# Side work of VectorE moved between slots, and three sets of loads moved ahead in SyncE's queue

## The chip, the cores and the metric

The kernel runs on one core of a Trainium2 chip. The metric is the device time of one execution in microseconds (us), the median of several runs. Engines: PE is TensorE, DVE is VectorE, ACT is ScalarE, POOL is GpSimd, SP is SyncE, which here only issues DMAs.

## The reference, cut to what matters

Two transformer-like blocks run one after the other on a sequence of 2048 tokens of width 1024, in float32. The change lies in the first block. It normalises x, projects it (`w_in`), and feeds one part of the projection to windowed attention and another, `u_ssm` (512 channels in 32 groups of 16), to a linear recurrence in both directions:

```
lam, dt  = a_re + i*a_im, exp(log_dt)
a_bar    = exp(lam * dt)
b_bar    = (b_re + i*b_im) * (a_bar - 1) / lam
xs       = scan(x_t = a_bar * x_{t-1} + b_bar u_t)      # 64 states a group, 2 directions
y       += Re(xs) c_re - Im(xs) c_im                      # plus d * u
```

## The kernel before, in words

All engines run programs written out by hand, with semaphores. Each engine works strictly in the order of its own program; SP, ACT and POOL also issue the DMAs.

**First projection (st).** `te_st` computes u and the gates by a seven-product scheme: 20 steps q = 0 to 19, each with products P1, P5, P6, P7, P2, P3, P4 of four 128x128 by 128x512 matmuls. P3 waits for the combination `c22` of the same step on DVE, P2 for `p1` of the same step on ACT. `ve_st` does for each q: `u2`, `c22` (two additions, u3 and c22), four sums of weights for q+1, side slot 2q, `c12`, `c21`, side slot 2q+1. So whatever stands in a side slot delays the combinations behind it. ACT makes gates of step q (behind c12 and c21), issues a weight load for q+2, and then makes p1 of q+1.

**Side slots.** `ve_side(v, s)` fills slot s with preparation of the recurrence: in slots 2 to 8 the parameters, the last of it the "turns" (`ve_prm_turns`, eleven rounds of up to ten small operations, each dependent on the one before), then eight quarters of matrices (`ve_mat`, quarter q4 in slots MAT_AT[q4] to +2, steps 0, 1, 2). Step 0 makes b1 and b2, step 1 six products for outputs and three for inputs, step 2 the other nine; step 2 ends with the event QA of the quarter. SP then stores the quarter to `pwd` in three DMAs (`sp_mat`), and loads coefficients of quarter q4+2 into the buffer BCs. `te_lag` multiplies 16 small matmuls of a quarter at the end of step q = LAG_AT[q4]; it waits for QA. `ac_lag` and `ve_lag` finish them (slot 2*LAG_AT[q4]+2), and SP stores them to `hkd`. POOL waits for the end of the turns and then makes the rotations (`po_rot`, 16 pairs of groups, about 34 us each), and stores them to `rotd`.

**Recurrence (s5).** For 32 groups g: `te_s5_first` transposes a loaded pwd matrix, `te_s5_states` multiplies it with Ug (u laid out by group, loaded from `ud` by `sp_ug`, m = 0 to 3 for eight groups each, eight copies of 128 KB a call), DVE rotates with the loaded rotation (`ve_s5_states`, L1170), scans, rotates back (`ve_s5_gates`, L1185), and `te_s5_out` multiplies the result. Late tiles of another projection (`te_proj`, weights loaded by ACT) are spread between the groups. SP issues all loads and stores of the stage in program order, `sp_s5`.

Of the kernel before, what the change touches and what calls it, by code (L numbers as in the profile page):

```python
# [23 lines left out]
TAILS = [48, 51, 54]  # L24
SP_, UT = 10, 4
SQ = 2 * SP_
MAT_AT = [9, 12, 15, 20, 23, 26, 29, 32]
LAG_AT = [6, 7, 10, 12, 13, 15, 16, 18]


class Counts:
# [62 lines left out]
def build(nc, T, out):  # L94
    ctx = ExitStack()
    with ctx:
# [5 lines left out]
        def reg(kb, *shape):  # L102
            o = int(round(kb * 256))
            n = 1
            for x in shape:
                n *= x
            assert o + n <= 207 * 256, (kb, shape)
            v = arena[:, o:o + n]
            if len(shape) == 2:
                v = v.rearrange("p (a b) -> p a b", a=shape[0])  # L110
            if len(shape) == 3:
                v = v.rearrange("p (a b c) -> p a b c", a=shape[0], b=shape[1])
            return v
# [472 lines left out]
        def ve_side(v, s):  # L586

            if s == 1:
                ve_bias(v)
            if s == 2:  # L590
                ve_prm_angle(v)
            if s == 4:
                ve_prm_coef(v)
            if s == 5:
                ve_prm_powers(v)
            if s == 6:
                ve_prm_turns(v, 0, 4)
            if s == 7:
                ve_prm_turns(v, 4, 8)
            if s == 8:  # L600
                ve_prm_turns(v, 8, 11)
            for q4 in range(8):
                if s == 2 * LAG_AT[q4] + 2:
                    ve_lag(v, q4)
            for q4 in range(8):
                if 0 <= s - MAT_AT[q4] < 3:
                    ve_mat(v, q4, s - MAT_AT[q4])

# [298 lines left out]
            s.do.dma_start(dst, pj_stage(n)).then_inc(*dma(f"st_sg{n % 2}", "pj", n))  # L907


        BCs = [reg(166.5, 4, 8, 16), reg(173.5, 4, 8, 16)]  # L910
        BAs = reg(175.5, 4, 256)
        CA2 = [reg(180, 4, 288), reg(114, 4, 288)]
        QAs = reg(184.5, 4, 288)
# [23 lines left out]
            s.do.dma_start(BCs[q4 % 2].rearrange("p a b c -> p (a b c)"), T["bc"][q4]).then_inc(*dma(f"ld_bc{q4 % 2}", "bc", q4))  # L937

        def sp_mat(s):
            sp_mat_load(s, 0)  # L940
            s.wait_ge(*at("prm_ve", "turns"))
            sp_mat_load(s, 1)
            for q4 in range(8):
                dst = pwd[4 * q4:4 * q4 + 4]
                s.wait_ge(*at("mat_ve", "QA", q4))
                s.do.dma_start(dst[:, :, 0:256].rearrange("g p n -> p g n"), BAs).then_inc(*dma("st_pw0", "pw", q4))
                s.do.dma_start(dst[:, :, 256:544].rearrange("g p n -> p g n"), CA2[q4 % 2]
                               ).then_inc(*dma("st_pw1", "pw", q4))
                s.do.dma_start(dst[:, :, 544:832].rearrange("g p n -> p g n"), QAs).then_inc(*dma("st_pw2", "pw", q4))
                if q4 + 2 < 8:  # L950
                    sp_mat_load(s, q4 + 2)
                if q4:
                    sp_lag(s, q4 - 1)
                if q4 in (2, 3):
                    sp_st_u(s, SP_ + q4 - 2, 0)
                    sp_st_u(s, SP_ + q4 - 2, 1)
            sp_lag(s, 7)
# [27 lines left out]
        def ve_lag(v, q4):  # L985
# [5 lines left out]
            tt(v, q, o, o, bank(7)[0:16, :].rearrange("p (g n) -> p g n", g=4)[:, :, 112:128], ADD)  # L991
            tt(v, q, o, o, dd, ADD, "H", q4)

        def ve_mat(v, q4, step):
            q = "mat_ve"
            c8_ = slice(8 * q4, 8 * q4 + 8)
            B1, B2, C1, C2 = (BCs[q4 % 2][:, k, :, :] for k in range(4))
            CAs, b1, b2, x2 = CA2[q4 % 2], b1s[q4 % 2], Bb[:, 0, :, :], Bb[:, 1, :, :]
            if step == 0:
                v.wait_ge(*at("prm_ve", "turns"))  # L1000
                v.wait_ge(*at(f"ld_bc{q4 % 2}", "bc", q4))
                v.wait_ge(*at("ld_sgn", "sgn"))
                v.wait_ge(*at("ld_dcol", "dcol"))
                ts(v, q, B2, B2, sgn[:, 1:2], None, MUL, BYP)
                ts(v, q, C1, C1, sgn[:, 0:1], None, MUL, BYP)
                ts(v, q, C2, C2, -1.0, None, MUL, BYP)
                cr, ci = bc(coef[:, 0, c8_], 2, [128, 8, 16]), bc(coef[:, 1, c8_], 2, [128, 8, 16])
                v.wait_ge(*at("side_pe", "H", q4 - 2))
                tt(v, q, b1, B1, cr, MUL)
                tt(v, q, x2, B2, ci, MUL)  # L1010
                tt(v, q, b1, b1, x2, ADD)
                tt(v, q, b2, B2, cr, MUL)
                tt(v, q, x2, B1, ci, MUL)
                tt(v, q, b2, b2, x2, SUB)
            if step == 1:
                pw_stored(v, q4 - 1)
                ve_mat_inputs(v, q4, 0)
                if q4 == 1:
                    v.wait_ge(*at("side_pe", "bias", 7))
                ve_mat_outputs(v, q4, 0)  # L1020
            if step == 2:
                ve_mat_inputs(v, q4, 1)
                ve_mat_outputs(v, q4, 1, "QA", q4)
# [268 lines left out]
        def sp_s5(s):  # L1292
            sp_ug(s, 0)
            for g in range(3):
                sp_s5_pw(s, g)
            sp_s5_blocks(s, 0)
            sp_s5_rot(s, 0)
            sp_s5_rot(s, 1)
            for n in LATE[0]:
                sp_proj(s, n)  # L1300
            for g in range(G):
# [13 lines left out]
                    sp_s5_channels(s, g)  # L1315
                for n in LATE[4 * g + 4]:
                    sp_proj(s, n)
                if g < 3:
                    sp_ug(s, g + 1)

# [2350 lines left out]
```

## Time and profile before

| what | value |
|---|---|
| median of 3 runs | 3506.26 us (3501.18 to 3506.35) |
| the profiled execution's own time | 3506.26 us |
| its span, first to last instruction | 3504.5 us |
| TensorE busy | 3373.6 us, 96% |
| VectorE busy | 1810.0 us, 52% |
| ScalarE, GpSimd busy | 1030.6 and 1151.2 us |
| mean granted TensorE clock | 0.989 |

Busy time counts instructions at work, not waits. The granted clock is a share of 2.4 GHz. The st stretch ends at 552.8 us, the recurrence follows.

### The profile page before, as it was taken

What the parts mean: (1) busy time and instruction counts of PE and PEld (TensorE: products, weight loads), DVE (VectorE), ACT (ScalarE), POOL (GpSimd) and SP (SyncE); (2) the same over time, 40 slices, a digit from 0 to 9 for tenths busy, and PEclk for the clock granted to TensorE, in tenths of its full rate; (3) what the DMA queues carried; (4) which work ended last, traced back from release to release, by engine and by line L of the source; (5) the groups of instructions that cost most, each with busy time, mean ns of one, the idle gap of its engine ahead of it and who ended that gap; (6) DMA issues with size and microseconds to landing.
All of it is one profiled execution on the core that took longest, in us unless ns stands there. A gap on an engine that the chain in (4) does not pass through costs nothing.

```text
span 3504.5 us, 32439 instructions
## 1 busy us (share of the span) xinstructions
PE 3373.6 (96%) x10992; PEld 1716.6 (49%) x10992; DVE 1810.0 (52%) x4003; ACT 1030.6 (29%) x2527; POOL 1151.2 (33%) x1499
## 2 busy tenths in 40 slices
PE   7999998999999999999999999999999996999998
PEld 4444444555445544444444445555664443444443
DVE  6778774665454773325565557744454554222222
ACT  3321222222100660002234446643332222322322
POOL 3087786750000890000000003655651001344342
PEclk9999999999999999999999999999999997999999
DMA  4344448655263103222221000000102226978885
GB/s 152 114 161 134 172 151 236 185 169 160 104 205 125 37 25 121 107 84 96 72 80 33 24 13 10 1 1 1 73 25 92 102 89 230 349 193 273 253 249 135
DMA packets 133161, 423.60 MB, mean 121 GB/s; under 512 B 20661, under 2 KB 60469, under 8 KB 116830
## 3 DMA queue, kind: packets, MB, share of 16 engines
q1 hardware_dynamic: 93388, 226.42, 19.3%
q0 software_dynamic: 31392, 153.50, 14.0%
q10 hardware_dynamic: 8208, 41.53, 3.4%
q8 instruction: 90, 1.47, 0.2%
q14 instruction: 83, 0.68, 0.1%
HBM read 354.96 MB, written 121.62 MB: 136 GB/s over the span
## 4 chain that ended last, share of the span: by engine, by line
PE 84%; DVE 8%; ACT 3%; DMA 2%; issue 1%; POOL 0%; SPq 0%; ACTq 0%; DVEq 0%; POOLq 0%
PE pst L145 55%; PE pst L383 10%; PE pst L150 6%; DVE arena L167 4%; PE pst L2619 3%; PE pst L2714 3%; PE pst L2622 2%; PE pst L1679 1%; DMA arena<-rotd 1%; PE pst L1594 1%; ACT arena L156 1%; PE pst L1152 1%; ACT arena L2459 1%; DVE arena L173 1%; DVE arena L170 1%
## 5 line engine op out<-in xcount | busy, mean ns | idle before, releaser
L145 PE MATMUL pst<-arena 128*128 128x512 f32 (+5 forms) x5290 | 2140.3, 560 | 22.9 <-DVE arena L1185 11.5
L145 PEld LDWEIGHTS pst<-arena 128*128 128x128 f32 (+1 forms) x5290 | 971.8, 191 | 1040.7 <-issue 999.1
L383 PE MATMUL pst<-arena 128*128 128x512 f32 x1120 | 489.3, 595 | 9.4 <-DVE arena L167 6.8
L167 DVE TENSOR_TENSOR arena<-arena 128x512 f32<-128x512 f32 (+9 forms) x897 | 455.1, 509 | 64.6 <-ACT arena L2660 19.6
L167 POOL TENSOR_TENSOR arena<-arena 128x4 f32<-128x4 f32 (+7 forms) x784 | 435.8, 556 | 81.4 <-DVE arena L2423 21.0
L150 PEld LDWEIGHTS pst<-arena 128*128 128x128 f32 x2080 | 244.3, 143 | 214.6 <-issue 149.3
L150 PE MATMUL pst<-arena 128*128 128x128 f32 x2080 | 310.1, 281 | 39.5 <-DVE arena L257 15.1
L383 PEld LDWEIGHTS pst<-arena 128*128 128x128 f32 x1120 | 211.4, 190 | 273.1 <-issue 253.4
L1647 POOL TENSOR_SCALAR arena<-arena 128x384 f32<-128x384 f32 (+1 forms) x128 | 151.5, 1202 | 399.2 <-DVE arena L1639 398.0
L156 ACT ACTIVATE arena<-pst,arena 128x128 f32<-128x128 f32 (+1 forms) x638 | 237.5, 470 | 138.0 <-PE pst L150 134.9
L2603 POOL TENSOR_SCALAR arena<-arena 128x512 f32<-128x512 f32 (+3 forms) x160 | 218.3, 1384 | 147.2 <-DVE arena L167 137.1
L173 DVE SCALAR_TENSOR_TENSOR arena<-arena 128x512 f32<-128x512 f32 (+4 forms) x438 | 198.2, 452 | 37.1 <-ACT arena L2122 19.4
L176 ACT ACTIVATE arena<-arena 128x1024 f32<-128x1024 f32 x64 | 67.6, 1056 | 502.3 <-DVE arena L1899 350.1
L173 DVE SCALAR_TENSOR_TENSOR arena<-arena,pst 128x256 f32<-128x256 f32 x96 | 43.3, 451 | 327.1 <-ACT arena L3344 325.4
L170 DVE TENSOR_SCALAR arena<-arena 128x1 f32<-128x1 f32 (+10 forms) x601 | 157.4, 262 | 95.2 <-ACT arena L2118 39.9
L155 ACT ACTIVATE arena<-pst 128x512 f32<-128x512 f32 (+4 forms) x242 | 121.3, 510 | 279.4 <-PE pst L145 112.4
L167 DVE TENSOR_TENSOR arena<-pst,arena 128x512 f32<-128x512 f32 (+2 forms) x156 | 103.3, 662 | 174.8 <-PE pst L383 96.5
L2024 POOL MEMSET arena<- 128x256 f32 x1 | 0.3, 311 | 476.8 <-ACT arena L156 476.8
L161 DVE COPY arena<-pst 128x512 f32<-128x512 f32 (+2 forms) x202 | 108.7, 545 | 79.1 <-PE pst L150 35.1
L2638 DVE TENSOR_REDUCE arena<-pst 128x2 f32<-128x1024 f32 (+2 forms) x80 | 85.3, 1066 | 114.2 <-PE pst L2622 113.1
L2714 PE MATMUL pst<-arena 128*128 128x256 f32 (+1 forms) x576 | 142.7, 371 | 1.2 <-DVE arena L161 1.2
L2654 ACT ACTIVATE arena<-pst,arena 128x512 f32<-128x512 f32 (+3 forms) x160 | 98.3, 619 | 143.0 <-DVE arena L2638 141.5
(217 smaller groups left out, 2407.6 us busy)
## 6 DMA issues: line engine op xcount, KB each, us to landing
arena<-in_w_ada SPq DMA_DIRECT2D x48, 512.0 KB, 4.7
arena<-in_w_ug ACTq DMA_DIRECT2D x18, 1024.0 KB, 6.0
sgd<-arena ACTq DMA_DIRECT2D x32, 512.0 KB, 3.4
rotd<-arena POOLq DMA_DIRECT2D x32, 512.0 KB, 4.7
arena<-rotd SPq DMA_DIRECT2D x32, 512.0 KB, 4.6
arena<-sgd SPq DMA_DIRECT2D x16, 1024.0 KB, 7.1
arena<-pwd SPq DMA_DIRECT2D x32, 416.0 KB, 5.8
arena<-in_x SPq DMA_DIRECT2D x18, 512.0 KB, 4.3
```

The lines of the kernel that those rows point to most:

```text
L145: x = t.do.matmul(o, l, r, start=(i == 0), stop=(i == len(pairs) - 1))
L150: x = t.do.transpose(o, i, ident[0:i.shape[0], 0:i.shape[0]])
L155: return a.do.activation(o, i, ACT.Copy)
L156: return a.do.activation(o, i, ACT.Identity, bias=0.0 if bias is None else bias, scale=1.0 if scale is None else scale)
L161: return v.do.tensor_copy(o, i)
L167: own(v, s).tensor_tensor(o, a, b, op).then_inc(*inc(s, *event))
L170: own(v, s).tensor_scalar(o, a, s1, s2, o1, o2).then_inc(*inc(s, *event))
L173: own(v, s).scalar_tensor_tensor(out=o, in0=a, scalar=sc, in1=b, op0=o1, op1=o2).then_inc(*inc(s, *event))
L383: x = t.do.matmul(st_bank(q, i), left[:, k, :], right[:, k, :], start=(name in FIRST and k == 0), stop=(k == 3), skip_group_check=name != ...
L1647: p.do.tensor_scalar(P_x, P_x, es[:, c:c + 1], None, MUL).then_inc(*inc("win_po", *(["P", j] if x == 3 else [])))
L2603: p.do.tensor_scalar(P_x, P_x, ff[:, r % 4, x, c:c + 1], None, MUL).then_inc(*inc("mla_po", "P", n, x))
L2714: last_ = t.do.matmul(bank(6 + x)[:, w], V2[:, 2 * hp + x, j, :], PT2[n % 4][:, 256 * l:256 * l + 256][:, w], start=(j == 0), stop=(j == 2 ...
```

## The change

The turns go into slots 6 and 7 instead of 6, 7 and 8. MAT_AT changes, so quarter 0 starts in slot 8 and quarters 5 to 7 one slot later; LAG_AT is computed from it and becomes 6, 8, 9, 12, 13, 15, 17, 18. The three input products of direction 0, and the wait for the stores of the quarter before, move from step 1 to step 0. The two buffers of coefficients change places, and the load of quarter 0 waits for the turns. In SP's program for s5 the Ug loads 1 and 2 are issued ahead of the first two rotation loads and Ug 3 right behind them, instead of after groups 0, 1 and 2.

```diff
-MAT_AT = [9, 12, 15, 20, 23, 26, 29, 32]
-LAG_AT = [6, 7, 10, 12, 13, 15, 16, 18]
+MAT_AT = [8, 12, 15, 20, 23, 27, 30, 33]
...
             if s == 6:
-                ve_prm_turns(v, 0, 4)
+                ve_prm_turns(v, 0, 6)
             if s == 7:
-                ve_prm_turns(v, 4, 8)
-            if s == 8:
-                ve_prm_turns(v, 8, 11)
+                ve_prm_turns(v, 6, 11)
...
-        BCs = [reg(166.5, 4, 8, 16), reg(173.5, 4, 8, 16)]
+        BCs = [reg(173.5, 4, 8, 16), reg(166.5, 4, 8, 16)]
...
         def sp_mat(s):
+            s.wait_ge(*at("prm_ve", "turns"))
             sp_mat_load(s, 0)
-            s.wait_ge(*at("prm_ve", "turns"))
             sp_mat_load(s, 1)
...
+        LAG_AT = [(m + 2) // 2 + 1 for m in MAT_AT]
...
                 tt(v, q, b2, b2, x2, SUB)
-            if step == 1:
                 pw_stored(v, q4 - 1)
                 ve_mat_inputs(v, q4, 0)
+            if step == 1:
                 if q4 == 1:
                     v.wait_ge(*at("side_pe", "bias", 7))
                 ve_mat_outputs(v, q4, 0)
...
             sp_s5_blocks(s, 0)
+            sp_ug(s, 1)
+            sp_ug(s, 2)
             sp_s5_rot(s, 0)
             sp_s5_rot(s, 1)
+            sp_ug(s, 3)
             for n in LATE[0]:
                 sp_proj(s, n)
...
                 for n in LATE[4 * g + 4]:
                     sp_proj(s, n)
-                if g < 3:
-                    sp_ug(s, g + 1)
```

## Rows read from the trace of the kernel before

**Rows 1.** The page, part 1: busy us, share of the span, instructions.

```profile
PE 3373.6 (96%) x10992; PEld 1716.6 (49%) x10992; DVE 1810.0 (52%) x4003; ACT 1030.6 (29%) x2527; POOL 1151.2 (33%) x1499
```

**Rows 2.** PE's waits in 110 to 552 us: total us, times, longest.

```profile
PE pst L383 <- DVE arena L167: 2.9, 3, 1.4
PE pst L383 <- ACT arena L155: 1.9, 1, 1.9
PE pst L972 <- DVE arena L167: 1.8, 1, 1.8
```

**Rows 3.** PE's waits in 552 to 720 us.

```profile
PE pst L145 <- DVE arena L1185: 8.6, 2, 6.8
PE pst L1152 <- ACT arena L155: 5.2, 7, 1.5
PE pst L150 <- DMA arena<-pwd: 3.6, 1, 3.6
```

**Rows 4.** PE's timeline: start, us, instructions, idle before and releaser.

```profile
244.16 1.92 PE L972 MATMUL pst<-arena 128*16 128x128 f32 x16 [1.75 <-DVE arena L167]
...
363.07 7.13 PE L383 MATMUL pst<-arena 128*128 128x512 f32 x16 [1.45 <-DVE arena L167]
...
466.00 10.57 PE L383 MATMUL pst<-arena 128*128 128x512 f32 x24 [1.87 <-ACT arena L155]
```

**Rows 5.** DVE and weight loads, 143 to 158 us; then L167 in one window.

```profile
143.53 1.49 DVE L167 TENSOR_TENSOR arena<-pst,arena 128x512 f32<-128x512 f32 x2
...
154.80 2.28 DVE L167 TENSOR_TENSOR arena<-pst,arena 128x512 f32<-128x512 f32 x3
...
157.14 0.41 PEld L383 LDWEIGHTS pst<-arena 128*128 128x128 f32 x2 [0.44 <-DVE arena L167]
...
160.75:166.39 5.64, 3.52 (x17) 0.00 (x0) 1.00 0.00 0
```

**Rows 6.** PE in 557 us (us, PE busy, clock, DMA share, GB/s), then PE's timeline.

```profile
557.00:558.00 1.00, 1.00 (x2) 0.50 1.04 421
...
556.67 8.73 PE L145 MATMUL pst<-arena 128*128 128x512 f32 x16
...
575.88 4.60 PE L145 MATMUL pst<-arena 128*128 128x256 f32 x10 [6.78 <-DVE arena L1185]
...
580.66 7.03 PE L145 MATMUL pst<-arena 128*128 128x512 f32 x16
...
588.40 2.32 PE L145 MATMUL pst<-arena 128*128 128x256 f32 x10
```

**Rows 7.** SP's queue, timeline from 545 us: start, us, issues.

```profile
545.25 3.66 SPq L661 DMA_DIRECT2D arena<-ud  x8
549.02 1.31 SPq L1106 DMA_DIRECT2D arena<-pwd  x3
...
554.19 0.86 SPq L1112 DMA_DIRECT2D arena<-rotd  x2
```

**Rows 8.** Landing of those two rotation loads, and DVE's timeline.

```profile
DMA to landing us min/median/max: 16.9/17.3/17.7
...
571.08 0.69 DVE L1170 TENSOR_TENSOR arena<-pst,arena 128x512 f32<-128x512 f32 x1 [3.87 <-DMA arena<-rotd]
```

**Rows 9.** A window while Ug 1 loads (last three: clock, DMA share, GB/s); queues in 560 to 572.

```profile
584.50:590.50 6.00, 6.00 (x22) 3.94 (x21) 1.68 (x3) 1.78 (x3) 5.11 (x12) 1.00 1.11 144
...
q10 hardware_dynamic: 239, 2.42, 52.7%
q1 hardware_dynamic: 555, 1.29, 28.6%
```

**Rows 10.** DVE's timeline near 219 and 362 us; landing of three pwd stores at 244.

```profile
219.05 11.72 DVE L167 TENSOR_TENSOR arena<-arena 128x512 f32<-128x512 f32 x9
...
362.33 0.69 DVE L167 TENSOR_TENSOR arena<-pst,arena 128x512 f32<-128x512 f32 x1 [3.40 <-DMA ud<-arena]
...
DMA to landing us min/median/max: 2.9/4.2/7.0
```

## The prediction

> **What bounds the kernel now.** The page's first part comes first: TensorE (PE) is busy for 96% of the span [rows 1]. So a change counts only where it moves a moment at which PE stands still. The change touches two stretches, the first projection (st, up to 552.8 us) and the start of the recurrence (s5, 552.8 to about 620 us). The second view is therefore the table of PE's waits in each [rows 2, 3]. In 110 to 552 us the reader sees 6.6 us that the change can reach: 1.8 for the lag product of quarter 1 (te_lag, L972), 2.9 in three waits of L383 for VectorE (DVE), and 1.9 in one for ScalarE. In 552 to 720 us PE waits 3.6 us for the first pwd load and 8.6 for DVE's gates, 6.8 of it at once. The third view is the timeline around these waits [rows 4 to 6], the fourth SP's queue and what it makes the gates wait for [rows 7 to 9].
>
> **Turns in two slots instead of three.** DVE's side work runs in slots, two for each step q. The change puts turns 4 and 5 into slot 6 and turns 6 to 10 into slot 7; before, the last three turns stood in slot 8, behind u2, u3 and c22 of q = 4. DVE is dense there: c12 and c21 of q = 3 run at 143.53, slot 7 ends as u2, u3 and c22 of q = 4 start at 154.80, these take 2.28 us, and product P3 of q = 4, which waits for c22, loads its weights at 157.14, 0.44 us late already [rows 5]. There is no cover left. The last three turns took 160.75 to 166.39, 5.64 us [rows 5]. They are the same 26 small operations (two rounds of ten and one of six) wherever they stand, so c22 of q = 4 ends 5.6 us later and P3 starts near 162.8: **+5.6 us**. The matmuls before it don't hide this: P2 runs before P3 already, and its own input (p1, which ScalarE makes behind the gates of q = 3) moves by the same 5 us and takes at most a part of the same wait. What is late next is c12 and c21 of q = 4 and sums of q = 5, but slot 8 now holds less that must be done before u2 of q = 5 and PE itself is late, so nothing is added.
>
> A wait of that length costs speed as well. After the 3.6 us wait at 552.8 the granted clock is 0.50, that is 1.2 instead of 2.4 GHz, at 557 us, and 16 records of 128x512 take 8.73 us where 16 at 580.66 take 7.03; after the 6.8 us wait 10 records of 128x256 take 4.60 where 10 at 588.40 take 2.32 [rows 6]. So 1.7 to 2.3 us. After waits of 1.8 us there is none of it: 24 records after the wait at 466.00 take 10.57 us, 0.44 each [rows 4]. The new wait of 4 to 5.6 us is nearest to the first: **+1.8 us**, with 0 and 2.3 as ends (0 if P2 splits it in two).
>
> The first load of the quarters' coefficients now waits for the turns, since its buffer lies on the parameters. It is 256 KB, with u2, u3, c22 and four sums between it and its user, over 5 us, so I put it at nothing; without that cover it would be 1 us, on DVE alone.
>
> **Quarter schedule.** For quarter 1 te_lag moves from the end of q = 7 to the end of q = 8, while its products still end in q = 7: the 1.75 us wait at 244.16 [rows 4] goes, and no later instruction takes it over, because u2 and c22 of q = 8 had 8 us of idle before them. **-1.8 us**. For quarters 3 and later, step 1 gives three of its nine products to step 0. The wait at 466.00 (ScalarE's p1, late because c12 and c21 of q = 15 stood behind the nine products of slot 31) loses the cause: **-1.9**. The three waits for DVE sum to 2.9 us; one of 1.45 is at 363.07, the other two together 1.4. These two go as the slots become shorter: **-1.4**. The one at 363.07 stays, because c22 of q = 12 waits for a store of ud at 362.33 that SP issues behind the quarter's stores [rows 4, 10]: 0, between -1.4 (slot 22 ends earlier) and +1.
>
> The move has a price. Step 0 now waits for pw_stored of the quarter before, and behind this wait stand u2, u3 and c22 of the next q. For quarters 2, 4, 6 and 7 the slot before step 0 is the one that ends the quarter before. The stores take up to 7.0 us from issue to landing [rows 10], and some 8 us with their issue. A product takes 3.5 us (16 records, two products, in 7.13 [rows 4]), and from the end of such a quarter to P3 of the next q PE has about five of them to do (P1, P5, P6, P7, P2), 17 us. The stores land at 8, so DVE's three products end near 10.5, and u2, u3, c22 near 13. It fits at q = 8 and, with a margin below 1 us, at q = 17, where quarter 6 ends late: **+0.3**, between 0 and 6 (four places at 1.5).
>
> Sum of the st stretch: 5.6 + 1.8 - 1.8 - 1.9 - 1.4 + 0.3 = **+2.6 us**.
>
> **The order of SP's loads.** Before, SP issues the eight copies of Ug 0 at 545.25, three pwd loads at 549.02, eight small block loads, and the first two rotation loads at 554.19 [rows 7]. The first rotation lands 16.9 us later, and DVE's first product (L1170) starts at 571.08 having waited for exactly it; DVE's gates end 4.8 us on, and PE starts at 575.88 [rows 6, 8]. The rotation load is thus on the path. The change puts Ug 1 and Ug 2, sixteen copies and 2.1 MB, ahead of it in the same queue. What such copies cost the engines shows where Ug 1 runs before: 584.5 to 590.5 us at 144 GB/s with the DMA engines' share at 1.11 [rows 9], so 1.05 MB takes 7.3 us, and two 14.6 us. That is the upper end. The lower is nothing: between 560 and 572 us SP's queue holds only 28.6% of the engines, and ScalarE's (the 2 MB of za's weights) 52.7% [rows 9], so part of the copies could run in the shadow of that load. But the engines are full all the while (1.04 at 557 us [rows 6]), so most of the copies' time must be added, not hidden; the row nearest to them is their own. If a quarter of the 14.6 us is hidden, 11 us are left. I take **+11 us**, with 5 to 14.6 as its own range. The clock penalty after this wait is already in the profile (2.3 us), so it adds nothing.
>
> The Trainium skill (DMA: Bandwidth & Descriptors, "Queues, rings and completion order") states that each DMA engine takes turns between the queues that have work, a packet at a time. The split of the three queues in this trace agrees; by that rule alone the weights of za don't hold SP's copies back, the delay would be nearer to 5 us than to 14.6, and the whole sum nearer to +8.
>
> Ug 3 goes behind the rotations, and rotation 2 behind it; DVE asks for it a whole group (10 us) after the gates of group 0, which covers 7.3 us. In the loop the three Ug calls disappear, 8 issues each. PE does not wait for any load between 576 and 620 us [rows 3], so their removal gives nothing.
>
> **Sum.** The profiled execution took 3506.26 us (its span 3504.5), which is also the median of the three runs. 3506.3 + 2.6 + 11 = 3519.9, said as **3519.5 us**.
>
> **Rivals.**
> *The Ug copies are hidden (not slower).* If the copies run wholly beside the za weights, the rotation lands when it did: +2.6 us and at most 3 of the rest, 3508 to 3511, within what can be told. For it: SP's share of 28.6%. Against: the engines' share of 1.0 and more in the same stretch. It decides from the point where the first rotation lands before 575 us in the old time frame.
> *DVE runs out of time in the late slots (slower still).* DVE and GpSimd disturb each other: nine products of two SBUF operands took 11.72 us at 219.05, 1.3 us each [rows 10], where a product of the same width at 571.08 takes 0.69 [rows 8]. GpSimd's rotation work starts 6 us earlier and meets DVE in other places. If step 0 comes late at four places, up to 6 us more: 3526. The Trainium skill (SBUF — State Buffer, "SBUF: two separate sides") says that the port pair which the two share is locked by one of them for a whole instruction; the 11.72 us bear it out, and it is as likely to help at one place as to hurt at another.
> *The turns fit (smaller loss).* If PE's wait at q = 4 is nil, the sum is 7.4 lower: 3512. Against it stand 0.44 us of wait already at that point.
> *The lighter queue pays (faster).* With the three Ug calls gone from the loop, PE's short waits for ScalarE in s5 (5.2 us in seven [rows 3]) could shrink. With hidden copies that is 2.6 - 5.2 = -2.6, 3504; it passes the bound of 7 us only if P3 of q = 4 does not wait either (-7.4 more): 3496. Against it: those waits are for a copy of ScalarE, not for a load.
>
> **How the numbers follow.** Forecast 0.60 (3513 to 3527, centre 3519.5), hidden copies 0.20, DVE late 0.10, turns fit 0.05, faster 0.05. Differences under 0.2% (7 us) can't be told from none here. Faster: 0.05. Same: the hidden copies and most of "turns fit", 0.23. Slower: 0.72. The range leaves out the faster case and the top of the two slow ones: 3507 to 3528.
>
> **What the profile after would show.** Right: P3 of q = 4 (with P2 ahead of it) waits 4 to 6 us for DVE near 157 us, with a granted clock of 0.50 behind it; no wait at te_lag of quarter 1; no wait of L383 for ScalarE near 466; L1170's first wait for rotd ends near 584 to 587 us and PE's wait for L1185 is 16 to 19 us instead of 6.8; nothing new between 600 and 900 us. Wrong: a rotation that lands within 20 us of its issue and ahead of the Ug copies, waits on DVE near 260, 363 and 488 us of more than 2 us each, or an end that moves by more than the s5 start does.

## The result

The changed kernel takes 3543.9 us (median of 4 runs, 3534.29 to 3552.55) against 3506.31 us (median of 4, 3501.18 to 3510.79): ratio 1.0109, 95% interval 1.009 to 1.0128, that is 32 to 45 us slower. The forecast was slower, 3519.5 us, with a range up to 3528: the direction was right, and the size, 13 us, was about a third of the 37.6 us that came. The profiled execution took 3544.84 us, its span is 3543.1 us.

The page of the changed kernel, part 1, answers to [rows 1]. PE has 7 us more of busy time (half clock), and the rest of the loss is idle:

```profile
PE 3380.4 (95%) x10992; PEld 1717.4 (48%) x10992; DVE 1811.2 (51%) x4003; ACT 1029.2 (29%) x2527; POOL 1147.4 (32%) x1499
```

PE's timeline of the changed kernel, to be held against [rows 4 to 6]. Columns are start, duration, instructions, and in brackets the idle time before and who ended it. L382 is what was L383, L969 is te_lag, L144 the matrix products of s5:

```profile
155.37 3.70 PE L382 MATMUL pst<-arena 128*128 128x512 f32 x8 [1.16 <-ACT arena L154]
163.80 5.91 PE L382 MATMUL pst<-arena 128*128 128x512 f32 x8 [4.73 <-DVE arena L166]
...
269.62 7.13 PE L382 MATMUL pst<-arena 128*128 128x512 f32 x16 [1.29 <-DVE arena L166]
276.68 1.92 PE L969 MATMUL pst<-arena 128*16 128x128 f32 x16
...
313.46 3.57 PE L969 MATMUL pst<-arena 128*16 128x128 f32 x16 [10.63 <-DVE arena L166]
316.96 73.34 PE L382 MATMUL pst<-arena 128*128 128x512 f32 x168
...
508.27 5.40 PE L382 MATMUL pst<-arena 128*128 128x512 f32 x8 [1.96 <-ACT arena L154]
518.40 9.53 PE L382 MATMUL pst<-arena 128*128 128x512 f32 x16 [4.73 <-DVE arena L166]
...
583.70 0.44 PE L149 MATMUL pst<-arena 128*128 128x128 f32 x2 [3.60 <-DMA arena<-pwd]
...
615.98 3.81 PE L144 MATMUL pst<-arena 128*128 128x256 f32 x10 [19.58 <-DVE arena L1184]
```

From this the loss can be put together, place by place (us):

| place | predicted | in this trace | how |
|---|---|---|---|
| P2 and P3 of q = 4 | +7.4 | +8.2 | 1.16 + 4.73 of wait; 5.91 for 8 records where 8 take 3.60 |
| te_lag of quarter 1 | -1.8 | -1.75 | no bracket at 276.68 |
| P3 of q = 8 (269.62) | 0 | +1.3 | |
| te_lag of quarter 2 (313.46) | 0 | +13.2 | 10.63 of wait; 3.57 instead of 1.92; 73.34 instead of the 72.37 that 168 records take |
| waits at q = 12 to 16 | -3.3 | -4.7 | all four gone |
| P2 and P3 of q = 17 | +0.3 | +10.9 | 1.96 + 4.73; 5.40 instead of 3.60; 9.53 instead of 7.13 |
| first gates of s5 | +11 | +12.0 | wait 19.58 against 6.78; 10 records in 3.81 against 4.60 |
| sum | +13.6 | +39.2 | spans differ by 38.6 |

PE ends the first projection at 580.1 us (583.70 less 3.60) instead of 552.8 and starts the first output product at 615.98 instead of 575.88. Two places, te_lag of quarter 2 and q = 17, show nearly the whole error of the forecast. Where a wait shows is not yet what makes it: the runs below give another sum by parts.

What the two places wait for is in DVE's timeline of the changed kernel:

```profile
294.16 18.60 DVE L166 TENSOR_TENSOR arena<-arena 128x512 f32<-128x512 f32 x17
312.86 0.21 DVE L166 TENSOR_TENSOR arena<-arena,pst 16x64 f32<-16x64 f32 x1
313.10 0.21 DVE L166 TENSOR_TENSOR arena<-arena 16x64 f32<-16x64 f32 x1
...
488.77 12.04 DVE L166 TENSOR_TENSOR arena<-arena 16x64 f32<-16x64 f32 x10
...
513.85 2.30 DVE L166 TENSOR_TENSOR arena<-arena 128x512 f32<-128x512 f32 x3 [8.85 <-DMA pwd<-arena]
```

The two 16x64 operations that end at 313.3 are `ve_lag` of quarter 1, and PE's te_lag of quarter 2 starts at 313.46: it waits for the event H of the quarter before (`side_ve`, "H", q4-1), not for its own products. With LAG_AT 8, `ve_lag` of quarter 1 stands in slot 18, behind the twelve differences T1, T2, T3 and the four sums that are made at q = 9 (17 operations with its own first, 18.6 us). With LAG_AT 9 for quarter 2, te_lag stands at the end of the same step. Near 500 us the three input products, now in step 0, start 8.85 us late because of the stores of quarter 6, and u2 and c22 of q = 17 stand behind them.

SP's queue at the start of s5 (columns as above, durations are of the issuing; answers to [rows 7]), and DVE's first product (to [rows 8]):

```profile
577.61 3.72 SPq L1120 DMA_DIRECT2D arena<-hkd  x8
581.44 15.03 SPq L658 DMA_DIRECT2D arena<-ud  x16
596.57 1.01 SPq L1111 DMA_DIRECT2D arena<-rotd  x2
597.68 9.46 SPq L658 DMA_DIRECT2D arena<-ud  x8
```

```profile
611.12 0.69 DVE L1169 TENSOR_TENSOR arena<-pst,arena 128x512 f32<-128x512 f32 x1 [15.71 <-DMA arena<-rotd]
```

The sixteen copies of Ug hold SP for 15.03 us, twice what 16 issues take when the queue is empty (8 in 3.66 us [rows 7]), so the rotation loads are not only served late but also issued late, at 596.57.

### The profile page after: what moved, and what is told of

Read it like the earlier page. It is cut to its first block, busy times and chain, and to the rows that moved or that the text cites. A ratio compares the mean times of both kernels' runs of the same rounds, so it can differ in the third digit from the quotient of the medians.

```text
span 3543.1 us, 32439 instructions
## 1 busy us (share of the span) xinstructions
PE 3380.4 (95%) x10992; PEld 1717.4 (48%) x10992; DVE 1811.2 (51%) x4003; ACT 1029.2 (29%) x2527; POOL 1147.4 (32%) x1499
## 3 DMA queue, kind: packets, MB, share of 16 engines
q0 software_dynamic: 31392, 153.50, 13.9%
q8 instruction: 90, 1.47, 0.2%
## 4 chain that ended last, share of the span: by engine, by line
PE 82%; DVE 9%; ACT 3%; DMA 2%; issue 1%; POOL 1%; SPq 1%; DVEq 0%; ACTq 0%; POOLq 0%
PE pst L144 54%; PE pst L382 10%; PE pst L149 5%; DVE arena L166 4%; PE pst L2619 3%; PE pst L2714 3%; PE pst L2622 2%; PE pst L1679 1%; DMA arena<-rotd 1%; PE pst L1594 1%; POOL arena L1647 1%; ACT arena L155 1%; DVE arena L169 1%; PE pst L1151 1%; DVE arena L172 1%
## 5 line engine op out<-in xcount | busy, mean ns | idle before, releaser
L144 PE MATMUL pst<-arena 128*128 128x512 f32 (+5 forms) x5290 | 2137.8, 560 | 33.9 <-DVE arena L1184 22.5
L144 PEld LDWEIGHTS pst<-arena 128*128 128x128 f32 (+1 forms) x5290 | 970.3, 191 | 1051.1 <-issue 1010.4
L382 PE MATMUL pst<-arena 128*128 128x512 f32 x1120 | 498.1, 604 | 18.6 <-DVE arena L166 14.7
L166 DVE TENSOR_TENSOR arena<-arena 128x512 f32<-128x512 f32 (+8 forms) x897 | 450.0, 503 | 73.1 <-ACT arena L2660 19.6
L382 PEld LDWEIGHTS pst<-arena 128*128 128x128 f32 x1120 | 214.5, 193 | 288.4 <-issue 257.7
```

The costliest lines, as they stand in the source:

```text
L144: x = t.do.matmul(o, l, r, start=(i == 0), stop=(i == len(pairs) - 1))
L166: own(v, s).tensor_tensor(o, a, b, op).then_inc(*inc(s, *event))
L382: x = t.do.matmul(st_bank(q, i), left[:, k, :], right[:, k, :], start=(name in FIRST and k == 0), stop=(k == 3), skip_group_check=name != ...
```

## The experiments

All differences are against runs of the kernel before on the same chip; its medians there were 3505 to 3506 us.

| run | from | edit | median us | ratio, 95% interval |
|---|---|---|---|---|
| a1_ug | before | SP's order only | 3521.77 | 1.0045 (1.0029 to 1.0062) |
| a2_turns | before | turns in slots 6, 7 only | 3519.66 | 1.0039 (1.0025 to 1.0053) |
| a3_lag89 | before | LAG_AT 8 and 9 for quarters 1, 2 | 3506.09 | 1.0003 (0.9993 to 1.0013) |
| a4_lag79 | before | LAG_AT 7 and 9 | 3506.75 | 1.0002 (0.9992 to 1.0011) |
| b1_lag10 | changed | LAG_AT 8 and 10 | 3536.88 | 1.0093 (1.0077 to 1.011) |
| b2_step1 | changed | input products back in step 1 | 3542.67 | 1.0109 (1.0092 to 1.0125) |
| b3_ugback | changed | SP's order back | 3531.76 | 1.0074 (1.0057 to 1.0091) |
| b4_turns3 | changed | turns in slots 6, 7, 8 | 3522.88 | 1.005 (1.0033 to 1.0066) |
| e1_sched | before | quarter schedule only | 3505.28 | 0.9998 (0.9988 to 1.0007) |
| h1_after_poollate | changed | GpSimd starts later | 3544.42 | 1.0118 (1.0101 to 1.0135) |
| f2_after_zalate | changed | load of za's weights later | 3537.87 | 1.0098 (1.0081 to 1.0115) |
| f1_before_zalate | before | load of za's weights later | 3501.07 | 0.999 (0.9981 to 1.0) |
| d1_s5order | before | another order of SP's loads | 3501.33 | 0.9989 (0.998 to 0.9999) |
| g1_best | before | f1, an order like d1, LAG_AT 8, 10 | 3497.50 | 0.9982 (0.9972 to 0.9992) |
| k1_lag10_ugback | changed | b1 and b3 together | 3523.54 | 1.0057 (1.0043 to 1.0071) |
| k2_turns_lag89 | before | a2 and a3 together | 3523.31 | 1.0054 (1.004 to 1.0067) |

Two further runs leave work out and are read by their first 600 us only.

### The parts alone

**a1_ug.**

```diff
             sp_s5_blocks(s, 0)
+            sp_ug(s, 1)
+            sp_ug(s, 2)
             sp_s5_rot(s, 0)
             sp_s5_rot(s, 1)
+            sp_ug(s, 3)
...
-                if g < 3:
-                    sp_ug(s, g + 1)
```

> Kernel before with only the order of SP's loads changed (Ug 1 and 2 ahead of the first two rotation loads, Ug 3 behind them). Theory: the rotation load waits in SP's queue behind 2.1 MB of copies into 16 partitions each; PE's wait for L1185 at the start of s5 grows from 6.8 to about 19.6 us as in the changed kernel, nothing comes back later: +12 to +13 us. Rival (copies hidden beside the load of za's weights): +0 to +3 us.

+16.3 us by the medians; the interval allows 10 to 22. The first projection is as before, and the wait for the gates is there, so the copies are not hidden. PE's timeline of a1_ug:

```profile
590.81 4.61 PE L145 MATMUL pst<-arena 128*128 128x256 f32 x10 [20.43 <-DVE arena L1185]
```

**a2_turns.**

```diff
             if s == 6:
-                ve_prm_turns(v, 0, 4)
+                ve_prm_turns(v, 0, 6)
             if s == 7:
-                ve_prm_turns(v, 4, 8)
-            if s == 8:
-                ve_prm_turns(v, 8, 11)
+                ve_prm_turns(v, 6, 11)
```

> Kernel before with only the turns in slots 6 and 7, all quarters where they were. Theory: P3 of q = 4 waits for c22, 1.2 us on ScalarE and 4.7 us on DVE, and some 2.3 us of half clock behind it: +8 us. Rival (later waits of the st stretch absorb it, since DVE has slack between q = 5 and q = 7): +0 to +4 us.

+14.2 us, more than the theory and against the rival. PE's timeline of a2_turns has the predicted pair at q = 4, and three waits behind it that are longer than in [rows 3, 4]:

```profile
156.70 3.70 PE L383 MATMUL pst<-arena 128*128 128x512 f32 x8 [1.15 <-ACT arena L155]
...
165.13 6.27 PE L383 MATMUL pst<-arena 128*128 128x512 f32 x8 [4.72 <-DVE arena L167]
...
256.23 3.29 PE L970 MATMUL pst<-arena 128*16 128x128 f32 x16 [3.38 <-DVE arena L167]
...
313.83 22.48 PE L383 MATMUL pst<-arena 128*128 128x512 f32 x48 [2.61 <-DVE arena L167]
...
571.94 0.69 PE L150 MATMUL pst<-arena 128*128 128x128 f32 x2 [7.05 <-DMA arena<-pwd]
```

The waits at q = 12 to 16 are gone in exchange. PE ends the first projection at 564.9 us, 12.1 later than in the kernel before.

**a3_lag89 and a4_lag79.**

```diff
-LAG_AT = [6, 7, 10, 12, 13, 15, 16, 18]
+LAG_AT = [6, 8, 9, 12, 13, 15, 16, 18]     # a3
+LAG_AT = [6, 7, 9, 12, 13, 15, 16, 18]     # a4
```

> Kernel before with only LAG_AT of quarters 1 and 2 changed, from 7 and 10 to 8 and 9. Theory: te_lag of quarter 2 at the end of q = 9 waits for ve_lag of quarter 1, which at LAG_AT 8 stands in slot 18, behind the twelve differences T1, T2, T3 and the sums of q = 9: a wait of about 10 us at the end of q = 9, 2.6 us of half clock, less 1.8 us of the wait at 244: +10 to +12 us. Rival (the wait is for the quarter's own products, which end later in the changed kernel): no wait here, -1.8 us.

> Kernel before with LAG_AT of quarter 2 alone moved from 10 to 9, quarter 1 stays at 7, so that ve_lag of quarter 1 is in slot 16, a step earlier. Theory (it is the neighbouring ve_lag that te_lag waits for): no new wait, the time of before within 3 us. Rival (quarter 2's products are late for the end of q = 9): a wait of several us at the end of q = 9.

The pair settles what te_lag waits for. In a3 it waits 6.07 us, behind the 17 operations and ve_lag of quarter 1; in a4, whose quarter 2 is at the same step, it waits for nothing. PE's and DVE's timelines of a3_lag89:

```profile
299.77 3.36 PE L972 MATMUL pst<-arena 128*16 128x128 f32 x16 [6.07 <-DVE arena L167]
```

```profile
285.03 13.90 DVE L167 TENSOR_TENSOR arena<-arena 128x512 f32<-128x512 f32 x17
299.04 0.21 DVE L167 TENSOR_TENSOR arena<-arena,pst 16x64 f32<-16x64 f32 x1
```

PE's timeline of a4_lag79:

```profile
295.81 1.92 PE L972 MATMUL pst<-arena 128*16 128x128 f32 x16
```

The time of a3 was a miss: +0.6 us where 10 to 12 were expected. The wait is real, but the 1.75 us at te_lag of quarter 1 and all four waits at q = 12 to 16 (4.7 us) are absent in its trace, and PE ends the first projection at 553.9 us against 552.8. Here a wait was exchanged for others nearly one for one.

### Parts undone in the changed kernel

**b1_lag10** sets `LAG_AT = [6, 8, 10, 12, 13, 15, 17, 18]`.

> Changed kernel with LAG_AT of quarter 2 back at 10 (6, 8, 10, 12, 13, 15, 17, 18), so that a whole step lies between the lag products of quarters 1 and 2. Changed kernel: 3544 us. Theory 1 (each wait stands by itself): the 10.6 us wait at the end of q = 9 and its 2.6 us of half clock go, 3531 us. Theory 2 (VectorE is what runs late, so a wait saved early comes back in part later, as the alone run of this piece was net nothing): some waits of L383 for VectorE come back between q = 11 and q = 16, 3535 to 3541 us.

7.0 us less than the changed kernel by the medians (the two intervals overlap), the time of theory 2, though not at its places. The 10.63 us wait is gone, and PE waits elsewhere instead: 4.34 us at 309.37 and 8.39 us at 515.16 (4.73 in the changed kernel). So PE ends the first projection at 576.7 us, only 3.4 us earlier.

**b2_step1** undoes the move of pw_stored and of the three products.

> Changed kernel with the wait for the stores and the three input products back in step 1. Theory (the wait for the stores of quarter 6 in slot 33 holds up u2 and c22 of q = 17): the 2.0 and 4.7 us waits of PE near 508 and 518 us and 4 us of half clock go, 3533 us. Rival (the slots are full wherever the three products stand): waits of L383 for VectorE appear at q = 13 to 16 as in the kernel before, 3540 us or more.

1.2 us less, inside the spread of the changed kernel: the time of the rival, but the waits at q = 13 to 16 that it named are not there. The theory falls in its size: P2 and P3 of q = 17 still wait 1.39 and 3.68 us (with half clock 7.7 us in all, 10.9 in the changed kernel), and te_lag 11.17. DVE now waits for a store of a gate tile instead of for the stores of quarter 6. PE ends the first projection at 575.5 us, 4.6 us earlier, and loses 3.3 of it again in a longer wait for the first gates (22.91 us). So the wait for the stores makes a part of the loss at q = 17, and not the larger one.

**b3_ugback** has SP's order of before.

> Changed kernel with the old order of SP's loads in s5. By the run of this piece alone (+16 us) and the growth of PE's wait for the gates (6.8 to 19.6 us): 3528 to 3532 us. Rival (the early loads pay where the start is late): 3538 us or more.

12.1 us less: with a1's 16.3 it gives 12 to 16 us for this part.

**b4_turns3** has `ve_prm_turns` in slots 6, 7 and 8 and MAT_AT[0] = 9.

> Changed kernel with the turns in slots 6, 7 and 8 again and quarter 0 in slots 9 to 11. Theory: the waits of P2 and P3 of q = 4 (1.2 and 4.7 us) and 2.3 us of half clock go, 3536 us. Rival (PE, no longer held up at q = 4, waits as much more at te_lag of quarter 2, since VectorE's work in q = 5 to 9 is the same): 3541 to 3544 us.

21.0 us less, where 0 to 8 were expected by either theory. PE's timeline of b4_turns3 shows that nothing is left at q = 4, half at te_lag and one short wait at q = 17, and DVE's shows why:

```profile
298.43 3.57 PE L971 MATMUL pst<-arena 128*16 128x128 f32 x16 [5.07 <-DVE arena L166]
...
496.16 8.83 PE L382 MATMUL pst<-arena 128*128 128x512 f32 x16 [2.27 <-DVE arena L166]
```

```profile
284.69 12.91 DVE L166 TENSOR_TENSOR arena<-arena 128x512 f32<-128x512 f32 x17
```

The same 17 operations take 12.91 us here and 18.60 in the changed kernel. They start 9.5 us earlier, and that is what PE lost at q = 4 and 8 (8.2 and 1.3). GpSimd stores a pair of rotations at 310.82 in the one and at 310.93 in the other (timeline of POOL), so in the changed kernel DVE's group, which follows PE, has moved into the end of GpSimd's pair, where its products are widest. This place of the group within GpSimd's pair is called the phase below. The groups by shape show it directly. The changed kernel in 302.1 to 311.1 us, DVE and POOL:

```profile
L166 DVE TENSOR_TENSOR arena<-arena 128x512 f32<-128x512 f32 x6 | 8.8, 1474 | 0.3
L166 POOL TENSOR_TENSOR arena<-arena 128x512 f32<-128x512 f32 x6 | 8.7, 1442 | 0.5
```

b4_turns3 in 284.7 to 291 us:

```profile
L166 DVE TENSOR_TENSOR arena<-arena 128x512 f32<-128x512 f32 x9 | 6.2, 692 | 0.9
L166 POOL TENSOR_TENSOR arena<-arena 128x32 f32<-128x32 f32 x4 | 2.9, 728 | 0.3
L166 POOL TENSOR_TENSOR arena<-arena 128x64 f32<-128x64 f32 x4 | 2.9, 728 | 0.3
```

Beside GpSimd's 128x512 products each of DVE's operations lasts about as long as GpSimd's (1.47 us against 0.69 alone); beside 128x256 it is 0.94 us (five in 295.9 to 301 us), beside the narrow ones 0.69. In the changed kernel six of the operations meet the widest products, in b4 none.

**e1_sched** is before with MAT_AT from b4, LAG_AT from b1, and the input products in step 0.

> Kernel before with the quarter schedule of the change alone: quarters 5 to 7 one slot later, input products and the wait for the stores in step 0, LAG_AT 6, 8, 10, 12, 13, 15, 17, 18; turns in three slots, SP's loads as before. Theory (this part is sound by itself, and the waits of the changed kernel come from the turns, the lag products of neighbouring steps and SP's order): no wait of 2 us or more for VectorE in the first projection, 0 to 5 us faster. Rival (the wait for the stores in step 0 costs where GpSimd disturbs): a wait near q = 17 of several us, 3 to 10 us slower.

No difference. The waits are 2.40 us at 363.79 and 1.39 us at 493.45; the theory's "no wait of 2 us" was a miss by 0.4, the rival's cost is not there. The quarter schedule with LAG_AT 10 for quarter 2 costs nothing by itself.

### GpSimd beside VectorE

**n1_after_norot and n2_before_norot** leave out the arithmetic of the rotations.

```diff
+                p.wait_ge(*at("st_pe", "P7", min(4 + q2, SQ - 1)))
-                own(p, q).memset(Ec[:, :, 0:1], 1.0).then_inc(*inc(q))
-                own(p, q).memset(Es[:, :, 0:1], 0.0).then_inc(*inc(q))
-                for j in range(8):
...
+                own(p, q).memset(Ec, 1.0).then_inc(*inc(q))
+                own(p, q).memset(Es, 0.0).then_inc(*inc(q, "rot", q2))
```

> Changed kernel whose GpSimd leaves out the arithmetic of the rotations: each pair of groups is two memsets and its two stores, paced by P7 of q = 4 to 19, so the output's recurrence part is not that of the reference. It shows the waits that remain when GpSimd does not work beside VectorE. Theory (part of the lateness is the sharing of VectorE with GpSimd): the 1.2 + 4.7 us at q = 4 stay (GpSimd does not work yet), te_lag of quarter 2 waits 6 us instead of 10.6, the waits near 508 and 518 us are under 2 us together, the first projection ends 10 to 15 us earlier than in the changed kernel; SP's queue makes PE wait 16 us or more for the first gates as before. Rival (the lateness is the number of VectorE operations alone): all waits as in the changed kernel within 1 us.

> Kernel before with the same left out (rotations are memsets and stores). Theory: the waits of PE at 363, 390, 441 and 466 us (4.7 us together) go, the one at te_lag of quarter 1 stays at 1 to 2 us, VectorE's nine-product groups all take about 6.9 us: 4 to 6 us less than before. Rival: they stay.

Only the first projection is read (in both, the part behind it is longer than in any other kernel here; the values that reach the later stages are others). In n1 te_lag waits 4.30 us and q = 17 nothing. PE ends the first projection at 560.5 us, 19.6 us earlier than in the changed kernel; 10 to 15 were expected. The waits at q = 4 are untouched. In n2 it ends at 546.8, 6.0 us earlier than before, with only te_lag's 1.74 us left. PE's and DVE's timelines of n1_after_norot:

```profile
305.05 3.57 PE L969 MATMUL pst<-arena 128*16 128x128 f32 x16 [4.30 <-DVE arena L166]
```

```profile
292.08 12.26 DVE L166 TENSOR_TENSOR arena<-arena 128x512 f32<-128x512 f32 x17
```

So the 17 operations need 12.3 us by themselves; GpSimd's arithmetic adds 0.6 in b4, 1.6 in a3 and 6.3 in the changed kernel. GpSimd's arithmetic costs this stage 19.6 us in the changed kernel and 6.0 in the kernel before. The changed kernel is 27.3 us later than the kernel before with it and 13.7 without it (560.5 against 546.8): half of the loss in this stage needs GpSimd at work.

**h1_after_poollate** delays GpSimd by one wait.

```diff
             p.wait_ge(*at("prm_ve", "turns"))
+            p.wait_ge(*at("st_pe", "P4", 4))
```

> Changed kernel whose GpSimd starts its rotations only behind P4 of q = 4, about 14 us later, which is where they stood against TensorE's steps in the kernel with the turns in three slots. Nothing is left out. Theory (VectorE's groups are long when they fall on GpSimd's long products, so the phase of the two decides): the 17 operations before te_lag of quarter 2 take 13 to 15 us instead of 18.6, the ten of quarter 6 about 7.5 instead of 12.0, PE waits 5 to 6 us at te_lag and under 4 us near q = 17: 3530 to 3536 us. Rival (the order of VectorE's operations after the early turns makes the groups late, whatever GpSimd does): 3541 us or more.

The total did not move (3544.4), so the forecast that a better phase would bring the 10 us back has failed. The waits moved: none is left at q = 17, but there are new ones, 2.59 at 221.63, 2.70 at 276.41, 3.75 at 393.50. At te_lag it is 8.83 with the 17 operations at 16.79 us. The delay did not last: GpSimd's first pair is stored at 204.6 us instead of 191.5, its fourth within 0.7 us of the time in the changed kernel. GpSimd did not catch up; the changed kernel's lost its lead, because it waited 10.40 us for the stores of its third pair where h1's waited 3.80. POOL's timelines, first h1_after_poollate, then the changed kernel:

```profile
311.59 1.48 POOL L1081 DMA_DIRECT2D rotd<-arena  x2 [0.30 <-POOL arena L166]
```

```profile
273.85 0.10 POOL L1062 MEMSET arena<- 128x4 f32 x1 [10.40 <-DMA rotd<-arena]
...
310.93 1.48 POOL L1080 DMA_DIRECT2D rotd<-arena  x2 [0.30 <-POOL arena L166]
```

So this run could not hold the phase apart at the place in question: six of the 17 operations again stand beside 128x512 products, though none beside 128x256. What it shows is that early waits can come in place of late ones, with the same total.

**k2_turns_lag89** puts a2 and a3 together, **k1_lag10_ugback** leaves the changed kernel with the turns and the quarter schedule alone.

> Kernel before with the early turns and LAG_AT of quarters 1 and 2 at 8 and 9, the quarter schedule and SP's order as before. The turns alone gave +14 us, this LAG_AT alone +0.6. Theory (the two meet: the later TensorE reaches q = 9, the more of the operations ahead of ve_lag fall on GpSimd's long products): +20 to +24 us, with a wait of 9 us or more at te_lag of quarter 2. Rival (they add up): +13 to +16 us, with a wait of 6 us.

> Changed kernel with SP's old order and LAG_AT of quarter 2 at 10: the early turns and the quarter schedule remain. Theory (the piece that costs with the turns is the wait of te_lag of quarter 2 for ve_lag of quarter 1): what is left is the cost of the turns alone, 3518 to 3524 us. Rival (the quarter schedule's own waits near q = 17 come with the turns): 3526 us or more.

k2: 17.3 us slower, between the theory (20 to 24) and the rival (13 to 16). Its te_lag waits 10.58 us, as in the changed kernel, where a3 without the turns waits 6.07; 18.55 us for the 17 operations. k1: 17.6 us slower, at the upper edge of its theory, with waits at q = 17 of 1.93 and 4.05 us; the turns alone have none there, the schedule alone (e1) one of 1.39. Beside the turns, each of the two neighbours costs 3 to 4 us, and alone next to nothing (0.6 in a3, none in e1). This is within the width of one interval (5 us) and is read from the waits, not from the medians.

### The start of s5

**f1_before_zalate and f2_after_zalate** issue the 2 MB load of za's weights on ScalarE's queue at group 5 instead of at 556 or 583 us.

```diff
                 k = 4 + q + 2 - SQ
+                if k == 5:
+                    return
...
+                if g == 5:
+                    a.do.dma_start(WS[PSLOT[5]], WSRC[PARTS[5]]).then_inc(*dma("ld_sw1", "pj", 5))
```

> Kernel before with the same load moved. Theory: the rotation load lands 5 to 6 us earlier, PE's wait of 6.8 us for the gates nearly goes, the clock penalty with it: 6 to 8 us faster. Rival: the wait stays above 4 us, less than 3 us faster.

> Changed kernel with the 2 MB load of za's weights issued at group 5 of s5 instead of at its start. Theory (the DMA engines serve SP's copies and this load one after the other, so each costs its full time): PE's wait for the first gates falls from 19.6 to about 14 us, 5 us faster than the changed kernel. Rival (the Ug copies are held up by their own 16 partitions and leave the engines room, so the load runs beside them): the wait stays above 18 us.

PE's wait for the first gates is 3.33 us in f1 (6.78 before) and 11.88 us in f2 (19.58 in the changed kernel). SP's queue in f2 issues the sixteen copies in 9.59 us instead of 15.03, timeline of f2_after_zalate:

```profile
582.37 9.59 SPq L660 DMA_DIRECT2D arena<-ud  x16
592.07 1.15 SPq L1113 DMA_DIRECT2D arena<-rotd  x2
```

The load does not run in the copies' shadow: it costs 7.7 us of wait beside the Ug copies and 3.5 without them. f1 is 4.2 us faster than before by the medians (interval 0 to 7), less than the 6 to 8 that was expected.

**d1_s5order and g1_best.** Before with this order of SP's loads, and (g1) with the za load late and LAG_AT of quarter 1 at 8:

```diff
-            sp_ug(s, 0)
-            for g in range(3):
-                sp_s5_pw(s, g)
-            sp_s5_blocks(s, 0)
-            sp_s5_rot(s, 0)
-            sp_s5_rot(s, 1)
+            sp_s5_pw(s, 0)
+            sp_ug(s, 0)
+            sp_s5_pw(s, 1)
+            sp_s5_rot(s, 0)        # g1: blocks ahead of both rotations
+            sp_s5_blocks(s, 0)
+            sp_s5_rot(s, 1)
+            sp_s5_pw(s, 2)
```

> Kernel before with another order of SP's first loads of s5: pwd 0, Ug 0, pwd 1, rotation 0, the block loads, rotation 1, pwd 2. If the order in SP's one queue sets both waits of PE at the start of s5, the first (3.6 us for pwd 0) goes with its 1.7 us of half clock, and the rotation lands some 3 us earlier: 6 to 9 us faster. Rival (the engines are full, whatever the order): the wait only moves to Ug 0 or to the gates, within 3 us of before.

> Kernel before with the pieces that gained: LAG_AT of quarter 1 at 8, za's weights late, and SP's order pwd 0, Ug 0, pwd 1, block loads, rotations 0 and 1, pwd 2. The two waits at the start of s5 (3.6 and 6.8 us with 4 us of half clock behind them) should nearly go: 8 to 12 us faster than before. Rival (waits of the first projection come back as in the other lag runs, and the engines stay full): within 4 us of before.

d1: 3.9 us faster (interval 0 to 7). The first wait falls from 3.63 to 0.99 us without half clock behind it. The second is as long as before, but for the block loads, which now come behind the rotation; PE's timeline of d1_s5order:

```profile
555.12 0.41 PE L150 MATMUL pst<-arena 128*128 128x128 f32 x2 [0.99 <-DVE arena L167]
...
572.27 4.29 PE L145 MATMUL pst<-arena 128*128 128x256 f32 x10 [6.16 <-DMA arena<-hkd]
```

g1 is 7.8 us faster than before (0.9982, interval 0.9972 to 0.9992), the only version here that clearly beats both kernels. PE starts the first output product at 564.88 us, 11 us earlier than before, after waits of 0.99, 1.49 and 3.33 us.

## Why the prediction was wrong

**The step that failed** is that each move was priced by itself, at its own place: behind the turns "nothing is added", and behind the quarter schedule "no later instruction takes it over". The parts show what stands in its place. The early turns, priced at 7.4 us (5.6 and 1.8), cost 14.2 us alone (a2) and 21.0 in the changed kernel (b4). The lag products, priced as a gain of 1.8, cost 0.6 us alone (a3), 3.1 on top of the turns (k2 less a2) and 7.0 in the changed kernel (b1; 8.2 by b3 less k1). The parts do not add up to one sum, because the cost of one depends on the others.

**The wait at te_lag.** The prediction looked at te_lag's own products alone. te_lag also waits for ve_lag of the quarter before, and the change puts quarters 1 and 2 at neighbouring steps, with DVE's heaviest block (T1, T2, T3 of q = 9) ahead of that ve_lag. In the trace 13.2 of the 25.6 us by which the sum was short stand here. It could have been read from the code: a3 and a4 differ in nothing but the slot of this ve_lag, and the wait is in the one and not in the other. But it is not worth 13.2 us: with the wait gone, b1 is 7.0 us faster, as other waits grow.

**The second term that was mis-sized** is the price of pw_stored in step 0: +0.3, between 0 and 6, measured 10.9 at q = 17. The place was named, "with a margin below 1 us, at q = 17", but the stores landed 13 us after the quarter's end, not 8 (quarter's products until 500.8, the three input products from 513.85), and the quarter itself ended late because the ten operations at 488.77, nine of them its own, took 12.04 us. b2 shows that the wait for the stores is only a part of it: without it the same two products still wait 5.1 us in all. It also varies: b1 and k1 are the same program up to s5, and DVE waits 12.64 us for these stores in the one and 6.56 in the other. n1 shows what is needed for the waits: without GpSimd's arithmetic those at q = 17 are nil.

**The turns.** Their local cost was right: +7.4 forecast, 8.2 found, split between P2 and P3 as the text allowed. What it missed comes later, at q = 9. Where the turns are early, the same 17 operations take 18.5 to 19.1 us (the changed kernel, b1, b2, b3, f2, k1, k2), but for h1 (16.79) and n1, without GpSimd's arithmetic (12.26); sixteen of them take 16.84 us in a2. Where the turns are not early, it is 12.9 to 13.9 us (b4, e1, a3), and 14.54 us for the sixteen in the kernel before. That GpSimd's work is needed for this is shown by n1, and that it is the phase which does it by the operations themselves: five or six of them stand beside GpSimd's 128x512 products in every run with early turns and GpSimd's arithmetic, none in b4, e1, a3 or the kernel before. How the one delay at q = 4 becomes 14 to 21 us at the end is shown by no single run; h1, meant to test it, did not keep the phase and didn't bring the time back.

**The rival "DVE runs out of time in the late slots"** was the right mechanism with too low a price (3526) and too low a chance (0.10). The forecast weighed it with 1.5 us a place. The Trainium skill (SBUF — State Buffer, "SBUF: two separate sides") has one engine hold the shared ports for a whole instruction; the operations that last as long as GpSimd's beside them agree with engines that block each other. They don't bear out a block for the whole instruction: six of each took 9.1 us together (302.1 to 311.2), where DVE's alone take 4.2 and GpSimd's 7.0 (b4, 303.9 to 310.6), 11.2 one after the other.

**The waits that went.** The forecast -1.8, -1.9 and -1.4 came as said, and the one at 363 us, which was to stay, went too. But in a3 and a2 they go as well, with none of the quarter schedule, and in e1 three of the four go with the schedule alone, while the one at 363 grows to 2.40 us. So the changed kernel does not show them to be savings of the new schedule, and e1 is no faster than the kernel before.

**SP's queue.** +11 was forecast, +12.0 read from the waits, 12 to 16 by a1 and b3. This is within the term's own range of 5 to 14.6. DVE's first wait for a rotation ends at 611.1 us, 27.3 of it the later end of the first projection; the 583.8 that is left is what was said (584 to 587). The prediction let a quarter of the copies' 14.6 us be hidden by the za load; f2 shows the reverse, the load takes 7.7 us from them. What was missing in the working is that SP itself stood: the issuing of the sixteen copies took 15.03 us, and the rotation loads were issued behind it. That a full queue held it is likely and not shown. From 581 to 597 us ScalarE's queue had 54.7% of the engines' time and SP's 49.6%, near to equal turns; so the Trainium skill's rule of turns between the queues (DMA: Bandwidth & Descriptors, "Queues, rings and completion order") is borne out as a split, but the +8 that was worked out by it is not, for both queues had work all the while. In [rows 9], 52.7% against 28.6%, the split agrees with the rule less well than the prediction says. What the removal of the three calls from the loop gave is shown by no run apart.

**What stays open.** Some 4 us of each interplay (k1, k2) lie within one interval. One trace is one execution: b1 and k1, the same up to s5, end the first projection at 576.7 and 569.0 us, so a place read from one trace can be off by several us. And no run holds GpSimd's phase fixed, since it moves with the landing of its stores.

## What to carry to other kernels

For every step that is moved, list all events that its first instruction waits for, those of its neighbours in the series included, and find the slot of each after the move; a chain across quarters (te_lag, ve_lag, te_lag) needs a distance, not only a date. Where an engine on the path waits a little at many places for another that is busy most of the time (DVE 327 of the 442 us from 110 to 552 in the kernel before), a wait removed at one place comes back at the next, and a delay put in early is not paid back later: price such a stretch by the fuller engine and by what works beside it. Bulk loads that are needed late belong behind the first load that is needed now, in the same queue and in every other.

## What the runs showed of the hardware that was not expected

Seventeen VectorE operations, nearly all of 128x512, took 12.26 us with GpSimd's arithmetic left out and up to 19.1 us with it. By the single operation, two SBUF inputs and 128x512: 0.69 us alone or beside GpSimd's products of up to 128x64, 0.94 beside 128x256, 1.47 beside 128x512. GpSimd pays as well: its 128x512 products took 1.44 us there and 1.17 with VectorE idle (b4). SP's issue of 16 copies of 128 KB took 15.03 us in the changed kernel where the load of za's weights was in flight, and 9.59 us where it was not; 8 such copies as the first of the stage took 3.66 us. In the rows of the first projection and of the first gates, waits of PE of 2.3 to 7 us were followed by 1.4 to 2.8 us of lost time (granted clock 0.50 in 163.80 to 166.80), longer ones by no more: 1.5 us after 19.58 (10 records in 3.81 us where 2.32 is the full-speed time), 2.3 us after 20.43 in a1. Near 2 us it goes either way: 1.8 us were lost after 1.96 in the changed kernel and nothing after 1.97 in b3, so the prediction's "none of it" after 1.8 us holds for its rows only. And in h1 GpSimd, started 13 us late, stored its fourth pair when the changed kernel's did, whose GpSimd had waited 10.40 us for a store.
